# Sixteen bytes of padding behind every feature tile of the projections' activations

## What is computed

```python
def first_block(x, ...):                       # x: (1, 256, 2048)
    proj = rms_norm(x, norm1_w) @ w_in         # 2048 x 5648: q, k, v, z, xbc, dt
    # q, k, v: 8 heads of 128, causal attention; z, xbc, dt: a Mamba-2 scan, 16 heads of 64
    x = x + concatenate([attn, ssm]) @ w_out   # 2048 x 2048
    u = causal_dwconv(rms_norm(x, norm2_w) @ w_up, ...)      # 2048 x 11264
    return x + (silu(u_gate) * u_val) @ w_down # 5632 x 2048

def second_block(x, c, ...):
    shift, scale, gate = split(silu(c) @ w_ada + b_ada, 3)
    h = rms_norm(x, g) * (1 + scale) + shift
    proj = h @ w_in_2                          # 2048 x 7168
    # 8 heads of dilated attention, 4 heads of two-way retention, gated
    return rms_norm(x + gate * (y @ w_out_2), final_gain)
```

## Time and profile before

| | value |
|---|---|
| runs | 1540.91 and 1541.81 us, median 1541.36 |
| span of the profiled execution, first to last instruction | 1537.5 us |
| a run's time beyond that span | 3.4 to 4.3 us |
| TensorE busy | 1524.5 us, 99% |
| VectorE busy | 1136.1 us, 74% |
| ScalarE busy | 778.1 us, 51% |
| GpSimd busy | 29.8 us, 2% |
| HBM read | 335.97 MB, 220 GB/s over the span |
| granted TensorE clock, mean | 0.998 |

### The profile page before, as it was taken

The page is one execution under the profiler, slowest core; times in us unless marked ns, Lnnn a source line. Parts: engine busy times, 40 slices in busy tenths (PEclk is TensorE's granted clock), DMA queues, the critical chain, the costliest instruction groups (busy, mean ns, idle before and its releaser), DMA issues. The chain is left out here.

```text
span 1537.5 us, 32072 instructions
## 1 busy us (share of the span) xinstructions
PE 1524.5 (99%) x12586; PEld 1483.7 (97%) x12586; DVE 1136.1 (74%) x1373; ACT 778.1 (51%) x930; POOL 29.8 (2%) x56
## 2 busy tenths in 40 slices
PE   9999999999999999999999999999999999999997
PEld 8999997999999999999999999999999989999997
DVE  7877777657987878788788887879854644764754
ACT  7645455545554444444444444445554643454554
POOL 0000000000000000000000000000000000000000
PEclk9999999999999999999999999999999999999999
DMA  9474556457877767677686776866465554445451
GB/s 348 171 272 161 200 177 220 146 171 273 302 282 249 288 233 273 244 249 274 235 293 229 262 272 221 300 219 217 150 247 194 196 193 162 160 159 185 154 186 58
DMA packets 85932, 339.23 MB, mean 221 GB/s; under 512 B 9680, under 2 KB 10208, under 8 KB 79328
## 3 DMA queue, kind: packets, MB, share of 16 engines
q1 hardware_dynamic: 77760, 281.05, 52.1%
q0 software_dynamic: 7232, 54.55, 10.1%
q10 hardware_dynamic: 864, 2.53, 0.4%
HBM read 335.97 MB, written 2.12 MB: 220 GB/s over the span
## 5 line engine op out<-in xcount | busy, mean ns | idle before, releaser
L683 DVE TENSOR_TENSOR wlo<-raw,whi 128x1024 fp32r<-128x1024 f32 x528 | 643.3, 1223 | 345.9 <-ACT whi L320 342.2
L320 ACT ACTIVATE whi<-raw 128x1024 fp32r<-128x1024 f32 x528 | 557.5, 1059 | 646.5 <-PE PS L1328 573.6
L1324 PE MATMUL PS<-gh,whi 128*128 128x256 f32 x3096 | 863.7, 279 | 0.7 <-DVE gl L1208 0.3
L1326 PE MATMUL PS<-gl,whi 128*128 128x256 f32 x3096 | 856.1, 277 | 0.0
L1328 PE MATMUL PS<-gh,wlo 128*128 128x256 f32 x3096 | 856.1, 277 | 0.0
L1324 PEld LDWEIGHTS PS<-gh,whi 128*128 128x128 f32 x3096 | 581.7, 188 | 5.9 <-issue 2.6
L1326 PEld LDWEIGHTS PS<-gl,whi 128*128 128x128 f32 x3096 | 581.4, 188 | 0.8
L1328 PEld LDWEIGHTS PS<-gh,wlo 128*128 128x128 f32 x3096 | 581.6, 188 | 0.0
L1324 PE MATMUL PS<-ah,whi 128*128 128x256 f32 x688 | 189.9, 276 | 0.0
L1328 PE MATMUL PS<-ah,wlo 128*128 128x256 f32 x688 | 189.9, 276 | 0.0
L1326 PE MATMUL PS<-al,whi 128*128 128x256 f32 x688 | 189.9, 276 | 0.0
(11 more groups left out here) (256 smaller groups left out, 894.6 us busy)
## 6 DMA issues: line engine op xcount, KB each, us to landing
raw<-weights SPq DMA_DIRECT2D x528, 512.0 KB, 3.6
ada_w<-w_ada POOLq DMA_DIRECT2D x48, 1024.0 KB, 5.9
EM<-rows POOLq DMA_DIRECT2D x1, 3072.0 KB, 12.4
X<-xT SPq DMA_DIRECT2D x3, 512.0 KB, 8.3
c<-const ACTq DMA_DIRECT2D x1, 1536.0 KB, 7.1
c_act<-c_rows POOLq DMA_DIRECT2D x1, 1024.0 KB, 7.0
outT<-X SPq DMA_DIRECT2D x2, 512.0 KB, 3.2
outT<-X SPq DMA_DIRECT2D x3, 256.0 KB, 2.2
```

The source lines that it names most:

```text
L320: act.activation(whi[:, j % SPLIT, :], raw[:, j, :], ACT.Copy).then_inc(s_hi, 1)
L683: dve.tensor_tensor(wlo[:, j % SPLIT, :], raw[:, j, :], whi[:, j % SPLIT, :].bitcast(F32), ALU.subtract).then_inc(s_lo, 1)
L1324: pe.matmul(out[:, t, :], whi[:, b, w], hi[:, kt, :], start=first and half == 0 and (apart or t % 2 == 0), stop=False, skip_group_check=True)
L1326: pe.matmul(out[:, t, :], whi[:, b, w], lo[:, kt, :], start=False, stop=False, skip_group_check=True)
```

## The change

The last dimension of the tensors behind `gh` and `gl` becomes 260 elements instead of 256, and the names `gh` and `gl` become views of the first 256. Tile k of each then begins at W + 192 + 16k modulo 256, and the sixteen tiles take the sixteen values once each. `gh` and `gl` each become 256 bytes longer per partition, so `gl` moves by 256 bytes and all that is placed behind by 512; no other tensor changes its place modulo 256. Nothing is issued, waited for or computed otherwise.

```diff
         at[0] += 192
-        gh, _ = place("gh", [P, DT, S], F32R)
+        ghp, _ = place("gh", [P, DT, S + 4], F32R)
+        gh = ghp[:, :, 0:S]
         at[0] += 0
-        gl, _ = place("gl", [P, DT, S], F32R)
+        glp, _ = place("gl", [P, DT, S + 4], F32R)
+        gl = glp[:, :, 0:S]
         at[0] += 192
```

## The result

The changed kernel takes 1574.51 us (two runs, 1574.32 and 1574.70) against 1541.36, 33 us or 2.15% more by these medians, where 12.5 us were forecast. The ratio of the runs is on record as 1.0221, with a 95% interval of 1.0203 to 1.0239: it is slower.

The account below looks back on a forecast made before the run. TensorE, busy 99% of a 1537.5 us span, was taken to bound the kernel through its matmul pace. Slow-pace matmuls, +16.6 us, less 4.1 already paid, gave +12.5: span 1550.0, plus 3.9 a run, 1554 us; range 1522 to 1584.

Parts of the forecast that it names:

- something is lost in every fp32r matmul: TensorE's reads: against 107.5 ns per 256 columns, matmuls lose 5.8 or 10.4 ns, by how two operand streams lie.
- the two paces: Same `gh`/`gl` matmuls in the trace before: 113.3 ns each in 40 blocks, 117.9 ns in 19, kept to block end.
- The first rival: TensorE's pace: nothing changes, since only instruction timing sets the state; 1541.4 us within 4, chance 0.31 (1537 to 1545).
- two independent ports: Skill page on TensorE: moving operand and weights are read separately, weight loads take no bandwidth; sum 0, time 1541.
- The 262 cycles: Skill page's issue gap for 256 columns when warm, 109.2 ns, set against the trace's 113.3 and 117.9 ns.
- I take that share, 0.32, for all tiles: `gh`, `gl`, `ah`, `al` matmuls: 19 of 59 blocks were slow, so 11520 x 0.32 x 4.5 ns = 16.6 us.
- The `ah` stretches: Matmuls with `ah` or `al`, 2112 in all: to inherit what the last `gh` tile left, slow share 0.32.
- The turned-round matmuls: 576 matmuls with moving weights and stationary `gh`, 228.9 ns for 512 columns: taken at 0, bounds -8 and +8 us.
- Writers and placement: ScalarE and VectorE conversions writing `gh`/`gl`, at most 4.5 us on an idle engine, and tensors moved by 512 bytes: nothing.
- The second rival: Place decides: slow pace is the rule away from W + 192; 39.7 + 9.5 - 4.1 us, 1586 us; above 1572, chance 0.14.
- 40 blocks of 59 come back to the fast pace: Trace before: of 59 blocks of at least 23 such matmuls, 40 ran at 113.3 ns; argued against place deciding.
- The test that I named: Timeline after, feed-forward part: 113/118 ns mixture for the forecast, 113.3 everywhere for no change, pace by tile number for rivals 2 or 3.

Follow-up runs that it names:

- residue 208: Against the kernel before the change: no padding, `gh` and `gl` as whole tensors 208 instead of 192 bytes from W modulo 256; 1587.52 us against 1539.92, 1.0305.
- the kernels at 64 and 208: Against the kernel before the change: unpadded `gh` and `gl` moved from W + 192 to W + 64, 1577.19 us (1.0236), or to W + 208, 1587.52 us (1.0305).

## Why the prediction was wrong

- **What bounds the kernel, and that the change acts on the pace alone: right.** Counts, clock and the other engines' busy times stayed; the whole difference is in TensorE's pace and reaches the end.
- **That something is lost in every fp32r matmul by the two streams' mutual place, and that the two paces are two states of it: right in the main.** The first rival, that only instruction timing is behind it, is refuted: with all else equal, 16 bytes move the time by 3% (residue 208). It would have given 1541 us. The prediction worked out the same 1541 from the two independent ports that the Trainium skill gives TensorE (TensorE: Matmul & The Clock Gate, section "Step-by-step: what each phase is for"). These runs don't show how the ports work; they do show that the places of both operands set the pace, which that section doesn't count. The 262 cycles that the prediction took from the Trainium skill (same page, section "Back-to-back issue gap") are given there for an isolated matmul, not for a stream with a weight load each, so 113.3 ns against 109.2 was by itself no sign of a loss.
- **The step that failed: "I take that share, 0.32, for all tiles".** I took a shift of place for the same thing as a shift of time, one more throw between the two known paces. It isn't. A block that starts at another time chooses between the paces that its place has; another place has other paces. Of sixteen places thirteen didn't have 113.3 ns in any of their blocks, so the slow share is not 0.32 but 13 in 16, and the slow paces are not one, 117.8, but 116.4 to 119.9. In numbers: `gh` and `gl` were to cost 9408 x 0.32 x 4.5 = 13.5 us and cost 9408 x 4.2 = 39.5. (The share itself was counted a little low. By the starts in the same trace 20 blocks of 59 are slow, with some 870 matmuls, if the one at 7.38 us in `product_first` is taken in; that adds about 1 us to the forecast and changes nothing.)
- **The `ah` stretches: wrong here, right elsewhere.** They were to inherit 0.32 of the slow pace, 3.0 us. They inherited nothing after the change, nor in the kernels at 64 and 208, where the stretches before them are slow, and they took the slow pace in every pass when `gh` or `gl` alone was padded. What decides between the two is open.
- **The turned-round matmuls**, taken at 0 within 8 us, cost 1.2 us. Writers and placement: nothing, as said.
- **The second rival, with 0.14, was the right one**, and its price, 39.7 us for `gh` and `gl` at 4.5 ns on 15 tiles of 16, was right to a microsecond, which is partly luck: 13 tiles are slow and not 15, and they lose 5.2 ns in the mean and not 4.5. Its 9.5 us for the `ah` stretches did not come, so its 1586 us were 11 too many. My argument against it, that 40 blocks of 59 come back to the fast pace, was no argument: all 59 had one place. The trace of before held no second place for this order, and I gave the chance to the case that it could show.
- The test that I named, a pace that belongs to the tile number, is what the timeline after shows.

## What to carry to other kernels

Where fp32r matmuls of 256 columns run back to back, read their pace from starts in the timeline and compare it with the same line elsewhere; durations hide it. If one line has two paces, the mutual place of the moving and stationary operands may be the reason; here it was a knob of up to 3%. Measure a bare loop of matmuls over the residues modulo 256 in steps of 16 bytes, with several starts for each, and choose the place that is fast behind all of them, for every order of operands that the kernel uses. Keep tile pitches a multiple of 256 bytes, and give all operands of one loop the same residue: spreading tiles over residues averages over mostly bad places.

## What the runs showed of the hardware

- The pace of an fp32r matmul of 256 columns with its own weight load is 113.3 to 121.5 ns by the operands' places (113.3 at distance 112, 120.0 and 121.5 four bytes beside it), with a granted clock of 0.998 and no other engine at work. Places that were fast behind every start tried: distance 112 with weights on an even multiple of 16 bytes, distance 192 with weights on an odd one.
- A place can have several stable paces (192: 113.3 or 117.8). Which one a block takes differs with what comes before it, by a rule that was not found, and it lasts while the places stay: in the kernel before, the block from 399 to 1096 us holds 113.3 ns for some 6100 matmuls.
- The least pace seen is 113.3 ns for 256 moving columns, 173.3 for 384 and 226.7 for 512. It doesn't shrink with 32 stationary columns instead of 128, but the places that have it change with that width and with the stationary operand's own place. What inside TensorE or its memory loses these cycles was not found; the runs only exclude the other engines, the DMA and the clock.
- With weight loads of 128 columns, no pace below 111.7 ns was seen, however few columns move.
